# Packed 128-row query and key sets, and a turned x stored once and read back, in a retention and sparse-attention step

## The reference, cut to what matters

```
h = rmsnorm(x, norm_g);  proj = h @ w_in              # 1024 columns in
rq rk rv rg (512 each) | aq (8 heads of 64) ak av (2 heads of 64) ag | iq (8 of 64) ik (64) iw (8)
ro = rmsnorm(retention(rope(rq), rope(rk), rv)) * silu(rg)
index[q, l] = sum over 8 heads of iw * relu(iq . ik[l])
sel = top 256 (or a quarter of the keys) of index, chunk-causal
ao = softmax over sel of (aq . ak) @ av, 4 query heads to a key head, * silu(ag)
y = rmsnorm(x + concat(ro, ao) @ w_out) * final_g
outputs: y, the retention states, k, v and indexer keys, for the prompt and for the sample
```

## Time and profile before

| what | value |
|---|---|
| runs | 972.59, 974.39, 982.64 us (median 974.39) |
| span of the profiled execution | 971.1 us |
| mean granted TensorE clock | 0.937 of full speed |
| TensorE (PE) busy | 873.8 us, 90% |
| VectorE (DVE) busy | 546.9 us, 56% |
| ScalarE (ACT) busy | 355.3 us, 37% |
| GpSimd (POOL) busy | 189.9 us, 20% |
| HBM traffic | 61 GB/s over the span |

### The profile page before, as it was taken

How to read it: one execution, slowest core, us unless ns; L and a number is a source line. 1 busy time by engine, 2 the same in 40 slices (tenths; PEclk the granted TensorE clock), 3 DMA queues, 4 the chain that set the end, 5 groups by cost and what they waited for, 6 DMA issues and landing times.

```text
span 971.1 us, 13082 instructions
## 1 busy us (share of the span) xinstructions
PE 873.8 (90%) x4413; PEld 709.0 (73%) x4413; DVE 546.9 (56%) x1337; ACT 355.3 (37%) x786; POOL 189.9 (20%) x374
## 2 busy tenths in 40 slices
PE   4789989989989999699898999999997999999983
PEld 3677767777767768567686778888876888888872
DVE  5433677696686867667532564544465644444422
ACT  5545464656364565546340121211124311111110
POOL 0333413222204031111002132222212011111100
PEclk9899998999999999869759899999997999999997
DMA  9210110102010000101224221111235432222121
GB/s 278 67 30 19 29 56 7 55 8 55 8 45 14 16 22 5 33 1 55 66 65 146 71 55 38 49 56 41 70 96 174 132 87 86 86 86 86 65 65 54
DMA packets 28273, 60.16 MB, mean 62 GB/s; under 512 B 7152, under 2 KB 9600, under 8 KB 28224
## 3 DMA queue, kind: packets, MB, share of 16 engines
q1 hardware_dynamic: 21920, 40.19, 15.1%
q0 software_dynamic: 6304, 19.36, 5.9%
HBM read 48.44 MB, written 11.09 MB: 61 GB/s over the span
## 4 chain that ended last, share of the span: by engine, by line
PE 62%; DVE 15%; issue 9%; ACT 5%; POOL 4%; DMA 3%; SPq 1%; DVEq 0%; POOLq 0%; ACTq 0%
PE bank L777 40%; PE bank L898 5%; PE bank L881 3%; PE bank L887 3%; PE bank L880 3%; DVE work L1413 1%; DVE top L1411 1%; DVE probs L1474 1%; PE bank L839 1%; PE bank L763 1%; DVE w_lo L1282 1%; PE bank L840 1%; DVE xT_lo L1317 1%; DMA stage<-in_w_out 1%; ACT pT L1117 1%
## 5 line engine op out<-in xcount | busy, mean ns | idle before, releaser
L777 PE MATMUL bank<-w_hi,xT_hi 128*128 128x512 f32 (+1 forms) x576 | 232.4, 403 | 13.9 <-DVE xT_lo L1317 9.6
L777 PE MATMUL bank<-w_lo,xT_hi 128*128 128x512 f32 (+1 forms) x576 | 226.2, 393 | 0.0
L777 PE MATMUL bank<-w_hi,xT_lo 128*128 128x512 f32 (+1 forms) x576 | 225.8, 392 | 0.0
L777 PEld LDWEIGHTS bank<-w_hi,xT_hi 128*128 128x128 f32 x576 | 111.9, 194 | 41.0 <-issue 12.7
L777 PEld LDWEIGHTS bank<-w_hi,xT_lo 128*128 128x128 f32 x576 | 111.6, 194 | 21.7
L777 PEld LDWEIGHTS bank<-w_lo,xT_hi 128*128 128x128 f32 x576 | 111.9, 194 | 19.6
L898 PE MATMUL bank<-v_sb,pT 128*128 128x64 f32 x648 | 98.7, 296 | 8.5 <-ACT pT L1117 8.0
L898 PEld LDWEIGHTS bank<-v_sb,pT 128*128 128x128 f32 x648 | 92.5, 216 | 15.4 <-ACT pT L1117 14.1
L1359 DVE SCALAR_TENSOR_TENSOR idx<-bank,iw_s,idx 128x384 f32<-128x384 f32 (+5 forms) x93 | 53.2, 610 | 41.5 <-ACT bank L1152 40.7
L1117 ACT COPY pT<-bank 128x512 f32<-128x512 f32 (+3 forms) x104 | 49.6, 494 | 66.1 <-PE bank L887 65.6
L887 PE MATMUL bank<-ident,probs 128*128 128x128 f32 x324 | 62.1, 309 | 9.5 <-ACT probs L1106 9.4
(11 more groups left out here) (186 smaller groups left out, 1386.8 us busy)
## 6 DMA issues: line engine op xcount, KB each, us to landing
xin<-in_x_prompt SPq DMA_DIRECT2D x48, 256.0 KB, 3.9
stage<-in_w_in SPq DMA_DIRECT2D x40, 256.0 KB, 2.7
early<-in_w_in SPq DMA_DIRECT2D x4, 1024.0 KB, 6.4
y_row<-in_x_prompt SPq DMA_DIRECT2D x16, 256.0 KB, 4.7
stage<-in_w_out SPq DMA_DIRECT2D x16, 256.0 KB, 3.4
out<-y_row POOLq DMA_DIRECT2D x8, 512.0 KB, 2.9
retained<-ro POOLq DMA_DIRECT2D x9, 256.0 KB, 2.4
mixed<-retained POOLq DMA_DIRECT2D x9, 256.0 KB, 3.1
```

Source lines behind the costliest of these rows:

```text
L777: mm = pe.matmul(out, (lo if which == 2 else hi)[:, k, :], (w_lo if which == 1 else w_hi)[slot][:, k, 0:width], start=(i == 0), stop=(i == ...
```

## The change

- **Queries**: q_row and aq_row hold each head once (ACT copies 128x512, POOL rotates 8 heads). One transpose turns a pair of heads, 4 transposes in place of 8. The even head lies in the upper 64 rows and the odd head in the lower; ACT rounds each into its half (two operations of 64x512), and DVE writes the rest into the other half (two operations of 64x512). So aqT now has both parts of a head in its 128 rows, as iqT had.
- **Keys**: kT becomes kT_hi and kT_lo, each with all 128 rows. A score is two full matmuls of 128 rows with one stationary operand aqT.
- **Cached keys**: POOL's doubling is gone, transposes are 4 in place of 8 and 8 in place of 16, and ACT and DVE write each half twice (DVE: 8 operations of 64x512 for the attention's keys in place of 4, 4 in place of 2 for the indexer's). The attention's cached keys are loaded into xin.
- **x**: xT_hi and xT_lo are one tensor xT of 1 MB to a tile. After each tile's turn in stage A, SP stores it to a DRAM tensor (`store_turned`); ACT's rounding of x(t+1) waits for that store. In stages R and O there is no load of x, no normalising and no turning: SP reads it back (`load_turned`) in two halves of 512 KB. Half 0 waits until the last product of the tile before (v in R, ag in O) is through its first 12 matmuls (`xT_half_used`), half 1 until that product is through.
- **Order**: the queue of SP is rewritten. x(R,2) now stands behind rg3 to rg7, the ag loads stand behind x(O,0), whose half 1 waits for v of the sample tile, and x(O,1) stands behind wo0's first seven.
- Scratch moves (rope_a and rope_b into spare weight columns, the square of x into probs), v's output is stored from v_sb, banks of R and O are renumbered.

```diff
-LATE = {(NT - 1, 1): ("aq", SAMPLE), (NT - 1, 2): ("x", TILES)}
+LATE = {(NT - 1, 1): ("aq", SAMPLE)}
...
+    xT_mem = nc.dram_tensor("turned_x", (TILES * P, 2, D), F32).ap()
...
-        kT = sb("kT", [P, KVH, NK], F32R)
+        kT_hi, kT_lo = (sb(f"kT_{x}", [P, KVH, NK], F32R) for x in ("hi", "lo"))
...
-        q_row = sb("q_row", [P, AH, 2, HD])
-        aq_row = sb("aq_row", [P, AH, 2, HD])
+        q_row = sb("q_row", [P, AH, HD])
+        aq_row = sb("aq_row", [P, AH, HD])
...
+            def store_turned(t):
+
+                wait_drained(sp, ("x1", "A", t))
+                sp.dma_start(xT_mem[t * P:(t + 1) * P, :, :], xT_raw)\
+                  .then_inc(xT_stored, 16)
+
+            def load_turned(phase, t):
+
+                for half in range(2):
+                    if isinstance(t, int) and (phase, t) == ("R", 0):
+                        if half == 0:
+                            wait_filled(sp, ("aq", "A", SAMPLE))
+                            sp.wait_ge(xT_stored, 16 * TILES)
+                    elif half == 0:
+                        sp.wait_ge(xT_half_used, spill_no(phase, t))
+                    elif isinstance(t, int) and t == 0:
+                        wait_filled(sp, ("v", "R", SAMPLE))
+                    else:
+                        wait_filled(sp, ("v" if phase == "R" else "ag", phase, t - 1))
+                    s = slice(half * BW, (half + 1) * BW)
+                    sp.dma_start(xT_raw[:, :, s],
+                                 xT_mem[bass.ds(t * P, P), :, s]).then_inc(xT_in[half], 16)
...
+            load_turned("R", 1)
             for k in range(STAGES, KD):
                 load(item_no["rg", k])
-            with sp.Fori(3, NT) as t:
-                load_x("R", t)
-            load_x("R", SAMPLE)
-            load_x("O", 0)
+            with sp.Fori(2, TILES) as t:
+                load_turned("R", t)
+            load_turned("O", 0)
             for k in range(KD):
                 load(item_no["ag", k])
-            load_x("O", 1)
             load_y(0)
-            for k in range(KD):
+            for k in range(KD - 1):
                 load(item_no["wo0", k])
-            load_x("O", 2)
+            load_turned("O", 1)
+            load(item_no["wo0", KD - 1])
...
-                        pe.matmul(out, aqT_hi[:, h, :], kT[:, kv, a:b], start=True, stop=False)
-                        pe.matmul(out, aqT_lo[r, h % (heads_of(t) // KVH), :], kT[r, kv, a:b], start=False, stop=True)\
-                          .then_inc(*fills(key))
+                        pe.matmul(out, aqT[:, h, :], kT_hi[:, kv, a:b], start=True, stop=False)
+                        pe.matmul(out, aqT[:, h, :], kT_lo[:, kv, a:b], start=False, stop=True).then_inc(*fills(key))
...
+            def hi_x(t):
+                if t:
+                    act.wait_ge(xT_stored, 16 * t)
                 for half in range(2):
...
+            def lo_queries(name, t, dst):
+
+                key = (name, "A", t)
+                for a in range(2):
+                    dve.wait_ge(hi_ready, hi_no(f"{name}{a}", "A", t))
+                    ins = dve.tensor_tensor(packed(t, dst, a, half_rows(1 - a)), turned_heads(t, key, a),
+                                            packed(t, dst, a, half_rows(a)).bitcast(F32), ALU.subtract)
+                ins.then_inc(*drains(key))
...
+            def lo_cached_keys(half):
+                key = ("turn_ck", half)
+                s = slice(half * BW, (half + 1) * BW)
+                dve.wait_ge(hi_ready, hi_no(f"ck{half}", "A", SAMPLE))
+                for g in range(KVH):
+                    for to in range(2):
+                        ins = dve.tensor_tensor(kT_lo[half_rows(to), g, s], of(key)[half_rows(g), :],
+                                                kT_hi[half_rows(g), g, s].bitcast(F32), ALU.subtract)
+                ins.then_inc(*drains(key))
...
                 rotate_q(t + 1)
                 decay_scores(t, dec_t)
-                normalise("R", t + 2)
                 rotate_k(t + 1)
                 retain(t, state, P)
-                lo_x("R", t + 2)
...
                 lo_mixed(t)
-                normalise("O", t + 2)
                 mix(t + 1)
-                lo_x("O", t + 2)
                 output(t)
```

More of the change, by code:

```diff
@@ L361, in hybrid_stream_step @@
         xn_ready = sem("xn_ready")
+        xT_stored = sem("xT_stored")
+        xT_in = [sem(f"xT_in{half}") for half in range(2)]
+        xT_half_used = sem("xT_half_used")
         hi_ready = sem("hi_ready")
@@ L433, in take_x @@
             for half in range(2):
-                take((f"x{half}", *x_of(t)))
+                take((f"x{half}", "A", t))
         take_x(0)
@@ L451, in hybrid_stream_step @@
                 take_rows(1)
-            take(("turn_aq0", "A", t))
-            take(("turn_aq1", "A", t))
-            for name, banks in (("turn_ci", 2 * (t == NT - 1)), ("turn_ck", 4 * (t == SAMPLE))):
+            take(("turn_aq", "A", t))
+            for name, banks in (("turn_ci", t == NT - 1), ("turn_ck", 2 * (t == SAMPLE))):
                 for b in range(banks):
@@ L458, in hybrid_stream_step @@
         base_r = list(uses)
[L459 to L465, removed]
+        R_BANK = {"q": 0, "k": 1, "v": 2, "kv": 3, "out": 4, "turn_q": 5, "turn_k": 6, "scores": 7}
+        base_o = [b + TILES for b in base_r]
+        O_BANK = {"rg": 0, "ag": 1, "y1": 2, "turn0": 5, "turn1": 6, "y0": 7}
         def bank_use(key):
@@ L519, in hi_no @@
                 return hi_at[s, phase, t]
[L520 to L526, removed]
+            return hi_o + int(s[-1]) + 2 * t + 1
         index_no, group_no, value_no, n, v = {}, {}, {}, 0, 0
@@ L580, in stat_no, with spill_no @@
         def stat_no(what, t):
[L582 to L586, removed]
-        def power_no(what, t):
[L590 to L598, removed]
+            return 1 + t if what == "y" else t
+        def power_no(what, t):
+            return {"A": 0, "retained": 1, "y": 1 + TILES}[what] + t
+        def spill_no(phase, t):
+            return t + (TILES if phase == "O" else 0)
         R_CONSTS = 16 * 5
         AO_STORES = 16 * (NT + 4)
-        NORM = {"A": 0, "R": TILES, "O": 2 * TILES}
         def slot_items(slot, what):
@@ L779, in product, with project @@
                                    start=(i == 0), stop=(i == PRODUCTS - 1))
+                    if last and i == PRODUCTS // 2 - 1:
+                        mm.then_inc(xT_half_used, 1)
                 if part[1] == PRODUCTS:
                     mm.then_inc(*fills(key))
-            def project(name, w, phase, t, first, part=(0, PRODUCTS), x=None):
-                product((name, phase, t), SLOT[w], WIDTH[w], xT_hi, xT_lo, w if first else None, part, x)
+            def project(name, w, phase, t, first, part=(0, PRODUCTS), x=None, last=False):
+                product((name, phase, t), SLOT[w], WIDTH[w], xT_hi, xT_lo, w if first else None, part, x, last)
             def turn_rows(key, rows, n):
@@ L971, in project_r @@
             def project_r(name, t, first=False):
-                project(name, f"r{name}", "R", t, first, x=("x", "R", t) if name == "q" else None)
+                project(name, f"r{name}", "R", t, first, x=("spill", spill_no("R", t)) if name == "q" else None,
+                        last=(name == "v"))
             def retain_tile(t, first=False):
@@ L1437, in between @@
             def between(name, t):
-                if name == "x":
-                    lo_x(*x_of(t))
-                elif name == "turn":
-                    for half in range(2):
-                        lo_below(t, (f"turn_iq{half}", "A", t), half)
+                if name == "turn":
+                    lo_queries("turn_iq", t, iqT)
                     key = ("turn_kv", "A", t)
```

359 lines of the change are left out of this document (156 added, 203 removed).

## The result

The changed kernel takes 926.87 us (923.67 to 930.36, 4 runs), the kernel before 973.89 beside it: a ratio of 0.9506, with a 95% interval of 0.946 to 0.9553. The profiled execution has a span of 922.1 us, 49.0 less than before.

What follows compares the result with a forecast made beforehand. TensorE, busy for 90% of the span, was taken as the bound. Stage A 23.3, start of R -1.7, R's loop 4.6, R to O -3.4 and O 5.2 sum to 28.0 us off 974.4: 946 us, range 930 to 966.

Steps and rivals of the forecast that it cites:

- Scores, the price of a pair: Attention scores: a 448-key pair takes 0.40 us instead of 0.77 at full clock; 384 keys 0.64 instead of 1.23 at half.
- Rival (b): Attention scores: the second weight load still waits, so about 8 us are saved, 966 us; chance 0.06.
- Scores, the term 12 x 0.6 = 7.2 us for the sample: Sample tile's attention: 12 score pairs each save 0.6 us at half clock, 7.2 us in all.
- rival (a): Sample's attention: gapless pairs raise the clock, and half-clock work loses 8 to 12 us more, 934 to 938; chance 0.20.
- The term 13.9 us for attend(4) to (7): Stage A: score pairs save 3.9, 3.6, 3.3 and 3.1 us, limited by VectorE's waits for scores; bounds 0 and 23.7.
- Cached keys: Stage A: VectorE's doubled operations cost 2.8 us before the sample's first score and 1.4 us for the indexer's keys.
- Stores of x: Stage A: the 9 stores of 1 MB are hidden, cost 0; at most 5 us if a store took 10.
- Read-back in R's loop: Stage R: six tile boundaries each save 1.1 us of turning less 0.35 of waiting for the load, 4.6 us.
- (c): Stage R: read-back late in every tile, landing at 7.4 us with cold restarts, 987 us; chance 0.08.
- (d): Read-back moderately late, landing at 5.5 us, or the weight ring's shift twice as dear, 960 us; chance 0.09.
- Start of R: Stage R's start: 4 us saved at x(R,1), but TensorE idles 5.7 us before q(2); net 1.7 us lost.
- the passage to O: Stage R to O: later ag loads idle TensorE about 12 us before scores(8); net 3.4 us lost.

Runs made afterwards that it cites:

- b_full_rows: Kernel before, with every second score matmul on all 128 rows (queries' high part twice, no low part): 937.59 us, ratio 0.9635.
- b_full_sample: Kernel before, with the full-row second score matmul (high part twice, no low part) in the sample tile's pairs alone: 960.95 us, ratio 0.9878.
- b_four_sample: Kernel before, with four full-row matmuls of the high part in place of each score pair of the sample tile: 961.41 us, ratio 0.9874.
- a_half_rows: Changed kernel, with the second score matmul put back on 64 rows: 958.06 us against 926.87.
- b_scale_later: Kernel before, with ScalarE's scaling of x of retention tile 0 moved behind the last relu of the sample's index: 967.62 us, ratio 0.9944.
- b_both: Kernel before, with both full-row second score matmuls (high part twice) and the later scaling of x: 932.83 us, ratio 0.9593.
- after_again: Changed kernel, unchanged, measured again beside the queue-order edits: 927.62 us, ratio 0.9522 to the kernel before.
- a_x2_first: Changed kernel, with the load of x(R,2) ahead of rg7 in SP's queue: 918.76 us, ratio 0.9439 to the kernel before.
- a_both_first: Changed kernel, with x(R,2) loaded ahead of rg7 and ag0 to ag4 ahead of x(O,0): 909.39 us, ratio 0.9331 to the kernel before.

## Why the prediction was wrong, by its own steps

**Scores, the price of a pair: right.** 0.64 us for 384 keys at half clock, and 0.39 to 0.49 for 448 at full clock where 0.40 was forecast; the pair before took 0.77. Rival (b) is out: the new second loads use the same rows and overlap, 0.7 us of idle in 108 of them where there were 23.1. The Trainium skill (TensorE: Matmul & The Clock Gate, Part 3, The mechanism) says in one place that a weight load overlaps only when the row groups differ, which these loads contradict; the same section also lets a load into the background weight buffer go ahead, and that agrees with them.

**Scores, the term 12 x 0.6 = 7.2 us for the sample: mis-sized.** It measured 13.0 us (43.7 to 30.7) in b_full_rows, since it was priced at a clock that the term itself changes. Where the clock rose late, in b_full_sample, it measured 7.5, so its size also hangs on when the clock rises. This was rival (a), at 0.20, in kind; it is 5.8 us more where (a) had 8 to 12, and 926.87 lies below the 934 of (a) too: 946 less this and the next two misses is 931, still inside the range, and some 6 us of smaller ones took the time out of it. b_four_sample shows the mechanism: under a denser stream the clock rises, whether or not TensorE has less to do.

**The term 13.9 us for attend(4) to (7): too small, too.** By b_full_rows it is 4.2 + 3.7 + 1.9 + 7.5 = 17.3. The first three (9.8 against 10.8 forecast) held. The excess is attend(7), 7.5 against 3.1, where half clock went from 17 us to 3.4. The size is uncertain: the kernel before has half clock for 27 us in that whole stretch, b_full_sample and b_four_sample, with the same instructions there, for 20 and 17, and a_half_rows for 7. The medians bear the excess out: all pairs give 35 us, the sample's alone 14 (5 to 19), so the others some 21, where 13.9 and about 2 were forecast. I had said that a clock that rises would do so in the sample's attention, and did not ask it of attend(7), though the trace had 0.50 there as well.

**A line of the diff not costed.** The condition `t != SAMPLE` on the scaling of x removes a wait of ScalarE in the sample's index, with 4.78 us of idle TensorE behind it. I took off x(R,0)'s turn and nothing for its scaling. b_scale_later prices it at 5 us (2 to 9), and b_both against b_full_rows at 5 as well.

These three are 5.8, 4.4 and 5 us, 15 of the 18 that stage A gave beyond the sum. The remaining 3 were not traced. Beside b_both the changed kernel saved 12.9 against 10.0 us in attend(4) to (6) and 13.4 against 11.2 in the stretch of attend(7), and it has fewer transposes there than b_both. In its second profile, after_again, the stretch of attend(7) is 60.5 us in place of 58.0, with half clock for 14 us in place of 10.

**Cached keys: right for the attention's, short for the indexer's.** VectorE's 8 operations take 5.6 us, and the time from the end of attend(7) to the sample's first score grew by 3.0 (2.8 forecast); the sample's index starts after 5.75 us of idle in place of 3.24, 2.5 more where 1.4 was taken.

**Stores of x: right.** The tightest, x(4)'s, was issued at 174.59 and takes 5.3; ScalarE rounds the next x at 181.99, with no wait for it.

**Read-back in R's loop: right.** Waits of 0.23 and 0.19 us at two of the boundaries and none worth a note at the others, where 0.35 was taken: 4.8 against 4.6 us (6 x 0.75 is 4.5; the recorded sum has 4.6). Rivals (c) and (d) needed landings of 5.5 us and more; in the loop they were 3.5 to 3.9. The sum by the Trainium skill (DMA: Bandwidth & Descriptors, Anatomy of one DMA), an estimate of 3.2 us for such a load, would have had no wait at all. The page fits it to DMAs that GpSimd issues, and these are SyncE's: the measured landing decides.

**Start of R and the passage to O: right in kind.** 6.89 us of idle for 5.7 forecast, 13.46 for 12, and -4.4 for -3.4. The two loads of x(R,2) landed in 5.0 and 5.4 us where 3.9 was taken, which is most of the 1.2 at q(2). a_x2_first and a_both_first show both causes as they were named, rg7's wait for a split and the ag ring behind v of the sample. The start of R gained 2.5 more than forecast: q(0) to scores(0), where x(R,1)'s turn and its wait for POOL lay, went from 34.6 to 26.9 us, 7.7 and not 4, and the idle ahead of q(2) took more back.

## What to carry to other kernels

Where a stretch runs at half clock, price an edit at both clocks: if it takes the gaps out of TensorE's stream, ask whether the clock that you price it with survives it, and in every stretch that shows 0.50, not in one. Look also at what the rest of a change does to the clock: this one gained it in the stretches that it was made for (42 us less at half clock) and lost nearly as much elsewhere (37 us more). The pair of matmuls that differ in rows left some 0.2 us at each weight load here, and filling both halves of the rows cost TensorE nothing here; it cost VectorE 2.8 us for the cached keys. When x or weights are read back through an in-order queue, put each load ahead of the first load in the queue that waits for something later than it does: two such moves gave 18 us here.

## What was not expected

- Twice the matmuls in the sample's scores, at 1.28 us for the pair's 1.23, made the stretch 11.5 us shorter (43.7 to 32.2), because the clock rose under them.
- The time of the kernel before spreads over 962.86 to 977.14 us in the 11 runs of one session that the ratio uses, and it follows the granted clock: 0.947 in the first of these, 0.930 in the last, which is half clock for 102 and 137 us. b_full_rows has 937.12 to 939.28 in 4 runs. In the profiles of before and of b_scale_later, which are the same kernel up to the sample's index, attend(4) takes 57.2 and 61.1 us, and the second has half clock from 242 to 253. So most of the spread of the kernel before is how long the clock is down. That the pairs steady it is not shown: b_both spreads over 5.9 us and the changed kernel over 6.7, in 4 runs each.
- The same unlike pairs ran at 0.50 through attend(7)'s first heads in the kernel before and in b_scale_later, and at 1.00 in a_half_rows. The granted clock there hangs on more than the pairs.
